# Second-layer attention of a decoder trunk: tokens reordered by two bits, a shared key block per half, values multiplied in TensorE from the other side, the gate turned in place of the output

## The reference

```python
for g, dil in enumerate((1, 4, 16)):                 # 16 heads of 128, 256 tokens
    s = q[g] @ k[g].T * 128**-0.5 - slope[head] * gap # gap = t_query - t_key
    valid = (gap >= 0) & (gap % dil == 0) & (gap // dil <= 128)
    lse_g, o_g = softmax_attention(where(valid, s, -1e30), v[g])
o = sum(softmax(lse)[g] * o_g)                        # per token and head
h = h + (o * silu(gate)) @ w_o
```

## Time and profile before

| | |
|---|---|
| median of 3 runs | 1440.93 us (1440.64 to 1441.14) |
| profiled execution, its own time | 1440.9 us |
| its span, first to last instruction | 1439.0 us |
| busy: PE, DVE, ACT, POOL | 1432.3, 847.1, 689.6, 109.9 us |
| instructions | 22314, of them 8008 matmuls and 8008 weight loads |
| granted TensorE clock | full in all 40 slices |

### The profile page before, as it was taken

One profiled execution on the slowest core, in us unless ns is written; L12 is line 12 of the kernel. 1 busy time (PEld: TensorE's weight loads), 2 busy tenths in 40 slices (PEclk: granted clock), 3 DMA queues, 4 the chain that ended last, 5 costly groups with the idle time before them and its releaser, 6 DMA issues.

```text
span 1439.0 us, 22314 instructions
## 1 busy us (share of the span) xinstructions
PE 1432.3 (100%) x8008; PEld 1252.1 (87%) x8008; DVE 847.1 (59%) x1229; ACT 689.6 (48%) x971; POOL 109.9 (8%) x68
## 2 busy tenths in 40 slices
PE   9999999999999999999999999999999999999998
PEld 6899999999888888888888888888888888888998
DVE  6767767749755556555556555646465555555553
ACT  6556555544344445444445444444444444454432
POOL 0100000000010002000101100200010110010000
PEclk9999999999999999999999999999999999999999
DMA  9654444454655645554554554464555455455453
GB/s 348 215 170 133 148 154 136 157 192 161 204 188 180 194 152 167 190 174 157 195 175 147 190 190 147 162 207 158 173 186 178 143 196 189 149 169 197 150 174 132
DMA packets 71218, 252.72 MB, mean 176 GB/s; under 512 B 7904, under 2 KB 8288, under 8 KB 71008
## 3 DMA queue, kind: packets, MB, share of 16 engines
q1 hardware_dynamic: 70704, 249.95, 52.4%
q10 hardware_dynamic: 432, 1.57, 0.3%
HBM read 249.40 MB, written 2.10 MB: 175 GB/s over the span
## 4 chain that ended last, share of the span: by engine, by line
PE 96%; DMA 1%; DVE 1%; issue 1%; ACT 0%; POOL 0%; SPq 0%; POOLq 0%; ACTq 0%
PE acc L1114 85%; PE turn L1144 3%; PE pv_bank L1156 3%; PE score L1351 2%; DMA raw<-in_w_in 1%; PE score L1243 1%; PE score L1245 1%; DVE w_lo L706 1%; PE turn L1229 0%; PE og_bank L1164 0%; ACT w_hi L441 0%; DVE xa_lo L847 0%; POOL rms L389 0%; ACT res L446 0%; PE pv_bank L1232 0%
## 5 line engine op out<-in xcount | busy, mean ns | idle before, releaser
L706 DVE TENSOR_TENSOR w_lo<-raw,w_hi 128x1024 fp32r<-128x1024 f32 x464 | 579.2, 1260 | 417.2 <-ACT w_hi L441 416.5
L441 ACT ACTIVATE w_hi<-raw 128x1024 fp32r<-128x1024 f32 x464 | 484.5, 1050 | 325.9 <-PE acc L1114 317.6
L1114 PE MATMUL acc<-w_hi,xa_hi 128*128 128x512 f32 (+1 forms) x1086 | 405.2, 373 | 0.9 <-DVE w_lo L706 0.8
L1114 PE MATMUL acc<-w_hi,xa_lo 128*128 128x512 f32 (+1 forms) x1086 | 396.7, 365 | 0.0
L1114 PE MATMUL acc<-w_lo,xa_hi 128*128 128x512 f32 (+1 forms) x1086 | 395.6, 364 | 0.0
L1114 PE MATMUL acc<-w_hi,xb_hi 128*128 128x512 f32 (+1 forms) x640 | 250.2, 391 | 0.0
L1114 PE MATMUL acc<-w_hi,xb_lo 128*128 128x512 f32 (+1 forms) x640 | 246.1, 385 | 0.0
L1114 PE MATMUL acc<-w_lo,xb_hi 128*128 128x512 f32 (+1 forms) x640 | 245.6, 384 | 0.0
L1114 PEld LDWEIGHTS acc<-w_hi,xa_lo 128*128 128x128 f32 x1086 | 204.7, 188 | 33.4
L1114 PEld LDWEIGHTS acc<-w_hi,xa_hi 128*128 128x128 f32 x1086 | 204.9, 189 | 32.5 <-issue 1.7
L1114 PEld LDWEIGHTS acc<-w_lo,xa_hi 128*128 128x128 f32 x1086 | 205.1, 189 | 30.9
(11 more groups left out here) (149 smaller groups left out, 947.5 us busy)
## 6 DMA issues: line engine op xcount, KB each, us to landing
raw<-in_w_b SPq DMA_DIRECT2D x320, 512.0 KB, 3.3
raw<-in_w_gate SPq DMA_DIRECT2D x32, 512.0 KB, 4.1
raw<-in_w_out_a SPq DMA_DIRECT2D x32, 512.0 KB, 3.3
raw<-in_w_out_b SPq DMA_DIRECT2D x32, 512.0 KB, 3.3
raw<-in_w_kv SPq DMA_DIRECT2D x16, 512.0 KB, 3.3
raw<-in_w_in SPq DMA_DIRECT2D x15, 512.0 KB, 6.3
raw<-in_w_q SPq DMA_DIRECT2D x16, 384.0 KB, 3.0
res<-in_x_tok SPq DMA_DIRECT2D x4, 512.0 KB, 8.0
```

The costliest lines, as they stand in the source:

```text
L441: nc.scalar.activation(w[0][:, s, 0:width], raw[:, s, 0:width], ACT.Copy).then_inc(hi_ready, 1)
L706: nc.vector.tensor_tensor(w[1][:, s, 0:width], raw[:, s, 0:width], w[0][:, s, 0:width].bitcast(F32), ALU.subtract).then_inc(lo_ready, 1)
L1114: last = nc.tensor.matmul(out, x(a), y(b), start=start and k == 0, stop=stop and k == 2, **more)
```

## The change

- Token order. The second layer's tokens lie by their two lowest bits: first bit (tile), second bit (half), then the rest. `token_order` gives it; the outputs of layer A are stored in that order (`later_order`, `of_tile`), the residual is loaded so from a second copy of the input (`xT_later`), `even_odd` is gone, and the final result is put back in order on the host side of the call.
- Scores. Keys of strides 4 and 16 lie now in the same 64-token half as the query. The score row is 64 + 64 keys for the second half of queries, 256 keys of stride 1, and 64 + 64 for the first half: still 512 columns of PSUM, of which each query half uses 384. The stride-1 product stays; each far stride is multiplied as two products of 64 key columns with the same stationary queries.
- The bias and maximum are done in two instructions of 64 partitions by 384; the exponential is 384 wide, and three blocks are transposed instead of four.
- Values. The values are the stationary side and the turned probabilities move, so the output comes out with the head dimension on the partitions and needs no transpose. Two products of 128 columns (stride 1) and two of 64 (one per query half, with strides 4 and 16 stacked along the partitions). For that the values of strides 4 and 16 are written by four instructions of 64 partitions per tile (`band_values`), in place of one.
- Gate. Gate times reciprocal of the sum (`band_gate`, VectorE) is transposed as a fourth block with the probabilities (`band_turn`), and VectorE multiplies the output by it (`band_out`). High and low parts are taken from that product (`band_store`, `band_low`). VectorE's stages in a step come in the order 3, 1, 2, 0.
- `phase`, the table that GpSimd halves once per pair, shrinks from 2048 to 1536 columns.

The core of the diff:

```diff
 def token_order():
-    return np.arange(SEQ).reshape(P, TILES).T.reshape(-1)
+    return np.arange(SEQ).reshape(HP, 2, TILES).transpose(2, 1, 0).reshape(-1)
...
+        def band_values(pair, t):
+            halves = (slice(0, HP), slice(HP, P))
+            return [(v[halves[g], t * 768 + (1 + half) * 256:t * 768 + (2 + half) * 256], halves[half],
+                     slice(g * 256, (g + 1) * 256)) for half in range(2) for g in range(2)]
...
ScalarE
                     if stage == 3:
-                        unit_store(U, i - 1, u)
+                        band_store((i - 1) * UNITS + u, i - 1, u)
                     if stage == 1:
-                        unit_turned(b_round(i, 1 + u), u, 512)
+                        if u:
+                            act.wait_ge(out_made, (i - 1) * UNITS + u)
+                        unit_turned(b_round(i, 1 + u), u, BAND + P)
                     if stage == 0:
-                        unit_exp(U, u, 512)
+                        unit_exp(U, u, BAND)
...
-                        nc.scalar.activation(v[:, 256:768], acc[:, pair, 0], ACT.Copy, scale=r[:, 0:1])\
-                            .then_inc(v_act, 1)
+                        for dst, src, cols in band_values(pair, 0):
+                            last = nc.scalar.activation(dst, acc[src, pair, 0, cols], ACT.Copy, scale=r[src, 0:1])
+                        last.then_inc(v_act, 1)
...
VectorE
+            def band_mask(U, B, u, bias, iteration):
+                dve.wait_ge(scored, U + 1)
...
+                for rows_at, first in ((slice(0, HP), P), (slice(HP, P), 0)):
+                    last = nc.vector.tensor_tensor_reduce(
+                        out=prob[rows_at, u % 2, 0:BAND], in0=score[rows_at, first:first + BAND], in1=bias[rows_at],
+                        scale=1.0, scalar=-3e38, op0=ALU.add, op1=ALU.max, accum_out=top[rows_at, u:u + 1])
+                last.then_inc(mask_done, 1)
...
+            def band_gate(U, u, g, gates_so_far):
...
+                dve.wait_ge(den_ready, U + 1)
+                nc.vector.tensor_scalar(og[:, u % 2], g, den_inv[:, u:u + 1], None, ALU.mult).then_inc(og_ready, 1)
+            def band_out(U, u):
+                dve.wait_ge(pv_ready, U + 1)
+                nc.vector.tensor_tensor(out[:, u % 2], pv, probT[:, BAND:BAND + P], ALU.mult).then_inc(out_made, 1)
...
-                for stage, u in b_units(s):
+                for stage, u in sorted(b_units(s), key=lambda unit: (3, 1, 2, 0).index(unit[0])):
                     if stage == 3:
-                        unit_low(U, i - 1, u)
+                        band_low(U, i - 1, u)
                     if stage == 2:
-                        unit_out(U, u, gate[:, 0, u % 2, (u // 2) * P:(u // 2 + 1) * P], i + PAIRS)
+                        band_out(U, u)
                     if stage == 1:
                         unit_den(U, u)
+                        band_gate(U, u, gate[:, 0, u % 2, (u // 2) * P:(u // 2 + 1) * P], i + PAIRS)
...
TensorE
+                nc.tensor.matmul(score[:, P:P + SEQ], qT[:, h * SEQ + t * P:h * SEQ + (t + 1) * P],
+                                 kT[:, h * SEQ:(h + 1) * SEQ], start=True, stop=True)
+                for g in (1, 2):
+                    col = (2 * g + h) * SEQ + t * P
+                    for half, first in ((0, P + SEQ), (1, 0)):
+                        at = first + (g - 1) * HP
+                        last = nc.tensor.matmul(score[:, at:at + HP], qT[:, col:col + P],
+                                                kT[:, col + half * HP:col + (half + 1) * HP], start=True, stop=True)
+            def band_turn(U, u, rnd):
+                pe.wait_ge(prob_ready, U + 1)
+                pe.wait_ge(og_ready, U + 1)
+                turn_rows(rnd, [(prob[:, u % 2, k * P:(k + 1) * P], k * P) for k in range(BAND // P)]
+                          + [(og[:, u % 2], BAND)])
+            def band_pv(U, B, u, rnd):
+                h, t = u // 2, u % 2
+                pe.wait_ge(turn_read, rnd + 1)
+                pe.wait_ge(out_made, B)
+                both = probT[:, 0:BAND].rearrange("p (a k) -> p a k", a=2)
+                for tile in range(TILES):
+                    nc.tensor.matmul(pv.rearrange("p (a k) -> p a k", a=2), v[:, tile * 768 + h * P:tile * 768 + (h + 1) * P],
+                                     both[:, :, tile * P:tile * P + HP], start=tile == 0, stop=False, skip_group_check=True)
+                for half, first in ((0, SEQ), (1, HP)):
+                    col = t * 768 + (1 + half) * 256 + h * P
+                    last = nc.tensor.matmul(pv[:, half * HP:(half + 1) * HP], v[:, col:col + P],
+                                            probT[:, first:first + HP], start=False, stop=True, skip_group_check=True)
...
                     if stage == 3:
-                        unit_turn_out(U, u)
```

More of the change, by code:

```diff
@@ L14 @@
 P = 128
+HP = P // 2
 SEQ = 256
@@ L133, with build_program @@
 N_MLA_CONSTS = CONST_COLS["sin"][1]
-N_PHASE = 2 * TILES * 512
+BAND = SEQ + P
+N_PHASE = 2 * TILES * BAND
 assert _at <= N_PHASE
-def build_program(nc, xT, x_tok, identity, consts, alibis, gains, w_in, w_pe, w_kv, w_gate, w_q, w_out_a, w_b, w_out_b, outT):
+def build_program(nc, xT, xT_later, x_tok, identity, consts, alibis, gains, w_in, w_pe, w_kv, w_gate, w_q, w_out_a, w_b, w_out_b, outT):
     ctx = ExitStack()
@@ L172, in build_program @@
         og = sb("og", [P, 2, P])
+        out = sb("out", [P, 2, P])
         ones = sb("ones", [P, 1])
@@ L304, in build_program @@
         o_ready = sem("o_ready")
+        out_made = sem("out_made")
         mask_begun = sem("mask_begun")
@@ L685, in b_pair, with band_store @@
                     highs((i, B_STEPS), B_0 + 5 + 2 * s, count=1)
+            def band_store(U, i, u):
+                act.wait_ge(out_made, U + 1)
+                act.sem_inc(store_begun, 1)
+                nc.scalar.activation(oT[0][:, bass.ds(i * 2 + u // 2, 1), (u % 2) * P:(u % 2 + 1) * P].rearrange(
+                    "p a k -> p (a k)"), out[:, u % 2], ACT.Copy).then_inc(o_hi, 1)
             q_gain = gn("q_group")
@@ L738, in unit_low @@
                 dve.wait_ge(o_hi, U + 1)
[L739 to L742, removed]
+                hi, lo = (later_order(x[:, bass.ds(i * 2 + u // 2, 1)], u % 2) for x in oT)
+                nc.vector.tensor_tensor(lo, of_tile(ogT), hi.bitcast(F32), ALU.subtract).then_inc(o_ready, 1)
             def stream_reduce(j):
                 dve.wait_ge(x_squares, j + 1)
-                out = reduced(j).rearrange("p (t m) -> p t m", t=TILES)
-                src = squares_of(j).rearrange("p c (m t) -> p t m c", t=TILES)
-                nc.vector.tensor_reduce(out, src, AX_X, ALU.add).then_inc(x_reduced, 1)
+                nc.vector.tensor_reduce(reduced(j), squares_of(j).rearrange("p c m -> p m c"), AX_X, ALU.add)\
+                    .then_inc(x_reduced, 1)
             def token_mean():
@@ L796, in chain_rows, with unit_mask @@
                     rms_of(units, span), ALU.mult)
-            def unit_mask(U, u, bias, width, iteration=None):
+            def unit_mask(U, u, bias, width):
                 dve.wait_ge(scored, U + 1)
-                if iteration is not None and u == 0:
-                    dve.wait_ge(alibi_ready, iteration + 1)
                 dve.sem_inc(mask_begun, 1)
@@ L809, in unit_mask, with band_low @@
                     .then_inc(top_ready, 1)
+            def band_mask(U, B, u, bias, iteration):
+                dve.wait_ge(scored, U + 1)
+                if u == 0:
+                    dve.wait_ge(alibi_ready, iteration + 1)
+                dve.sem_inc(mask_begun, 1)
+                for rows_at, first in ((slice(0, HP), P), (slice(HP, P), 0)):
[3 more added lines that the diff above has]
+                last.then_inc(mask_done, 1)
+                dve.wait_ge(mask_done, U + 1)
+                nc.vector.tensor_scalar(top_neg[:, u:u + 1], top[:, u:u + 1], -1.0, None, ALU.mult)\
+                    .then_inc(top_ready, 1)
+            def band_gate(U, u, g, gates_so_far):
+                if u == 0:
+                    dve.wait_ge(gate_done, gates_so_far)
+                dve.wait_ge(den_ready, U + 1)
[3 more added lines that the diff above has]
+                nc.vector.tensor_tensor(out[:, u % 2], pv, probT[:, BAND:BAND + P], ALU.mult).then_inc(out_made, 1)
+            def band_low(U, i, u):
+                dve.wait_ge(o_hi, U + 1)
+                hi, lo = (x[:, bass.ds(i * 2 + u // 2, 1), (u % 2) * P:(u % 2 + 1) * P].rearrange("p a k -> p (a k)")
+                          for x in oT)
+                nc.vector.tensor_tensor(lo, out[:, u % 2], hi.bitcast(F32), ALU.subtract).then_inc(o_ready, 1)
             def unit_den(U, u):
@@ L1083, in b_pair @@
                         dve.wait_ge(slot_used, i * B_STEPS + (B_0 + 32))
-                        nc.vector.tensor_scalar(v[:, 768 + 256:2 * 768], acc[:, (B_FILL_0 + par + V12) % 2, 1], r[:, 1:2],
```

(30 more changed lines are left out.)

43 lines of the change are left out of this document (19 added, 24 removed).

## The result

The changed kernel takes 1468.57 us (median of 4 runs, 1468.29 to 1468.77) against 1440.89: a ratio of 1.0192, 95% interval 1.0174 to 1.0210: slower, clear of noise, and by about 2%. The forecast was 1471 within 1451 to 1481.

What follows compares the result with a forecast made beforehand. TensorE, busy 1432.3 of 1439.0 us, was taken to bound the kernel. Count 10.75 plus waits 18.6 gave 29.4 us on 1440.9, 1470.3, rounded up to 1471 for the possible hold; range 1451 to 1481.

Steps and rivals of the forecast that it cites:

- rival A: Waits before TensorE's turns are hidden and only the instruction count matters: 1451.7 us, chance 0.12.
- Part 1: TensorE's count per unit: four instructions more at 0.111 us each, one transpose less, +10.75 us for 32 units.
- Part 2: TensorE's turns of probabilities wait for VectorE's gate in the second layer: +18.6 us, bounds 0 and about 30.
- possible hold: VectorE's second half mask may start only when earlier instructions finish: about 0.07 us per unit, some 2 us, outside the sum.
- Part 3: Costs taken as nothing: half-height value copies, strided writes, natural-order stream, reordered residual load, shorter GpSimd halving, dropped waits.
- B: Half-width float32 matmuls on TensorE cost by columns: 1429 us, chance 0.07, or 1453 with waits, chance 0.04.

Runs made afterwards that it cites:

- e1_gate_early: Changed kernel with a unit's reciprocal and gate moved directly behind its bias-and-maximum in VectorE's program: 1450.05 us.
- e4_before_cut: Kernel before, with each of its two 128-column far score products cut into two of 64 columns: 1455.66 us.
- e3_both: Changed kernel with each far stride's scores in one 128-column product, plus the edit of e1_gate_early: 1435.56 us.
- e7_one_mask: Changed kernel with one bias-and-maximum instruction of 128 partitions by 384 in place of two half-height ones: 1458.50 us.
- e6_values_more: Changed kernel with two more half-height value copies each on ScalarE and VectorE per pair, six for four: 1468.50 us.
- e5_gate_later: Changed kernel with one spare multiplication on VectorE ahead of the gate's: 1474.27 us.
- e8_early_spare: Kernel of e1_gate_early with one spare multiplication on VectorE ahead of the gate's: 1450.09 us.
- e9_alternate: Kernel of e3_both with the value products ordered near, far, near, far instead of near, near, far, far: 1435.43 us.

## Why the prediction was right

**Direction and size.** Both terms were there: waits 17.8 us against 18.6, count 9.2 against 10.75 (e1_gate_early, which has no wait left, less the kernel before). With the 0.7 us that the waits cost beyond themselves, that is the measured 27.7 against 29.4 forecast. The stated range alone would not have told this: rival A's 1451.7 lies in it too. It is the two terms, each measured by itself, that bear the mechanism out.

**Part 1, the count.** The price of a 64-column instruction, bracketed between one column and 128, held: 0.11 (e4_before_cut: 0.114). The wrong part is small: I took the value block as eight full pitches. In fact the pair of 64-column products ahead of the transposes ends one half pitch early, 0.055 x 32 = 1.8 us, which is the difference between 10.75 and 9.2 up to 0.2, and between the -3.5 and the -5.5 of e3_both up to 0.2. In the score that half pitch is given back by the projection that follows.

**Part 2, the waits.** Counted from the first projection after the score, the turns opened at 634.32 - 627.91 = 6.41 for unit 0 (forecast 6.37) and 643.65 - 636.03 = 7.62 for unit 1 (7.69). Waits of 0.82, 1.21, 0.10 and 0.11 stand against 0.8, 1.2 and 0.1 to 0.2 twice, and in the last pair 0.57 and 1.57 against 0.5 and 1.6. Bias and maximum took 1.18 to the next instruction (628.33 to 629.51) for the supposed 1.20. e7_one_mask takes 0.58 out of it, more than the 0.44 that the change had put in, so its 9.6 us tell only roughly what the lengthening alone cost. Two small errors stood against each other: the reciprocals came earlier than forecast (5.76 for 5.82 at unit 0, 7.05 for 7.14 at unit 1), and from a reciprocal to its turn it was longer (0.65 and 0.57 for 0.55), as the gate's multiplication has 0.29 for 0.25. The possible hold between the half-height instructions (the Trainium skill, VectorE: DVE Perf Modes, section Two Vector instructions with no wait between them) can't be told apart: the second starts 0.57 after the first, which is 0.55 long, but a read-out of the maximum lies between them as well.

**Part 3** held: e6_values_more; the first score of the second layer starts at 502.0 in both kernels; and from the last turn of probabilities to the end of the span it is 66.0 before and 65.8 after.

**What I had wrong in how it would show.** I expected the idle time to be put down to VectorE. The profile says "issue". The turn now waits for two semaphores, which may be why no releaser was found; no run tests that. Without e5_gate_later and e8_early_spare that name would be an argument only.

**The rivals.** A (waits hidden) is refuted by the 16 idle turns and by e1_gate_early, which is the kernel in which A is true: 1450.05, for A's 1451.7. B (by columns) is refuted by e4_before_cut. The figure of 25 ns for 1 to 64 columns (the Trainium skill, TensorE: Matmul & The Clock Gate, section Back-to-back issue gap) was no argument for B: the section gives it for a single matmul by itself and says that at small widths it leaves out the weight load. Its section LDWEIGHTS, by which loading 128 columns takes an estimated 107 ns, agrees with the 0.114 of e4_before_cut.

## What to carry to other kernels

Where float32 matmuls of 128 columns or fewer follow each other, each with its own weight load, count instructions, not columns: cutting a 128-column product in two doubled its price here, and a strided output made the cut needless. When a step of a busy engine gets a new operand from another engine, look up what stands ahead of that operand's instruction in its own engine's program; a producer that is idle 40% of the time can still be late by its order. Moving two instructions into an idle gap ahead of the long ones removed all of these waits here.

## What the runs showed of the hardware

A half-height bias-and-maximum (64 partitions by 384) takes 0.55 us, as long as a full-height one of the same width (0.56 in e7_one_mask): halving the partitions gains nothing. A transpose's weight load followed the last load of a 64-column float32 product after 0.06 us, half the usual 0.11. The weight loads of e1_gate_early show it, four at 0.11 and then the turn's:

```profile
639.02 0.53 PEld L1424 LDWEIGHTS pv_bank<-probT,v 128*128 128x128 f32 x4
639.41 0.37 PEld L1192 LDWEIGHTS turn<-ident,prob 128*128 128x128 f32 x3
```

The fourth starts at 639.36, the turn's at 639.41. The load of a 128-column product behind a 64-column one came after the full 0.11 in e9_alternate.
